# A two-layer decoder trunk on one core: expert weights in transfers of two pieces, and gathered tokens turned by VectorE instead of TensorE

## What is computed

```python
def swiglu(x, wg, wu, wd):
    return (jax.nn.silu(x @ wg) * (x @ wu)) @ wd

def moe(xn, w_router, wg, wu, wd):          # xn: 256 tokens x 2048, RMSNorm of x
    t = xn.reshape(-1, D)
    logits = (t @ w_router).astype(jnp.float32)
    top_vals, top_idx = lax.top_k(logits, TOP_K)            # 2 of 8
    gates = jax.nn.softmax(top_vals, axis=-1)
    comb = jnp.einsum('nk,nke->ne', gates, jax.nn.one_hot(top_idx, N_EXPERTS, dtype=jnp.float32))
    y = jnp.zeros_like(t)
    for e in range(N_EXPERTS):
        y = y + comb[:, e:e + 1].astype(t.dtype) * swiglu(t, wg[e], wu[e], wd[e])
    return y.reshape(B, S, D)
```

## Time and profile before

| | us |
|---|---|
| median of 3 runs | 1911.96 (1910.83 to 1913.84) |
| the profiled execution, its own time | 1910.22 |
| its span in the profile | 1908.5 |
| PE busy | 1897.8 (99% of the span) |
| DVE busy | 1440.1 (75%) |
| ACT busy | 1165.3 (61%) |
| POOL busy | 137.2 (7%) |
| HBM read and written | 495.33 MB and 13.64 MB, 267 GB/s over the span |

### The profile page before, as it was taken

How to read it: one execution, slowest core, us unless ns; L and a number is a source line. 1 busy time by engine, 2 the same in 40 slices (tenths; PEclk the granted TensorE clock), 3 DMA queues, 4 the chain that set the end, 5 groups by cost and what they waited for, 6 DMA issues and landing times.

```text
span 1908.5 us, 25748 instructions
## 1 busy us (share of the span) xinstructions
PE 1897.8 (99%) x8912; PEld 1580.5 (83%) x8912; DVE 1440.1 (75%) x1862; ACT 1165.3 (61%) x1490; POOL 137.2 (7%) x152
## 2 busy tenths in 40 slices
PE   9999999999999999999999999999999999999998
PEld 7888888888888888888888888888888888888887
DVE  8886677547764676566569678898988989888896
ACT  7656644434443444334545667888787878787885
POOL 8300000000000000000200010000000100010101
PEclk9999999999999999999999999999999999999999
DMA  9655566666666666665565468999999999999997
GB/s 358 195 159 164 177 193 193 191 196 192 194 191 195 192 195 190 196 193 187 185 186 167 145 217 337 374 397 385 396 386 398 379 398 378 403 378 403 375 396 258
DMA packets 141572, 510.13 MB, mean 267 GB/s; under 512 B 15937, under 2 KB 15953, under 8 KB 140081
## 3 DMA queue, kind: packets, MB, share of 16 engines
q1 hardware_dynamic: 134288, 486.64, 72.0%
q0 software_dynamic: 7200, 22.39, 4.6%
HBM read 495.33 MB, written 13.64 MB: 267 GB/s over the span
## 4 chain that ended last, share of the span: by engine, by line
PE 98%; DMA 1%; issue 0%; DVE 0%; ACT 0%; POOLq 0%; SPq 0%; DVEq 0%
PE main L637 31%; PE main L639 31%; PE main L638 31%; PE transpose L974 1%; PE transpose L655 1%; PE transpose L1014 0%; DMA raw_pieces<-in_ffn_moe 0%; PE transpose L957 0%; PE transpose L677 0%; DMA raw_pieces<-in_w_in 0%; PE transpose L732 0%; PE transpose L733 0%; PE transpose L731 0%; PE transpose L744 0%; PE spread L712 0%
## 5 line engine op out<-in xcount | busy, mean ns | idle before, releaser
L1423 DVE TENSOR_TENSOR w_low<-raw_pieces,w_high 128x1024 fp32r<-128x1024 f32 x919 | 1099.4, 1223 | 310.9 <-ACT w_high L1075 301.8
L1075 ACT ACTIVATE w_high<-raw_pieces 128x1024 fp32r<-128x1024 f32 x919 | 952.3, 1059 | 293.6 <-DMA raw_pieces<-in_ffn_dense 167.9
L637 PE MATMUL main<-w_high,xT_high 128*128 128x512 f32 (+1 forms) x1856 | 717.5, 387 | 0.3 <-DVE w_low L1544 0.2
L639 PE MATMUL main<-w_high,xT_low 128*128 128x512 f32 (+1 forms) x1856 | 709.7, 382 | 0.0
L638 PE MATMUL main<-w_low,xT_high 128*128 128x512 f32 (+1 forms) x1856 | 708.9, 382 | 0.0
L639 PEld LDWEIGHTS main<-w_high,xT_low 128*128 128x128 f32 x1856 | 348.8, 188 | 68.5
L637 PEld LDWEIGHTS main<-w_high,xT_high 128*128 128x128 f32 x1856 | 349.1, 188 | 66.3 <-issue 1.4
L638 PEld LDWEIGHTS main<-w_low,xT_high 128*128 128x128 f32 x1856 | 349.3, 188 | 65.3
L637 PE MATMUL main<-w_high,hT_high 128*128 128x512 f32 x832 | 329.9, 396 | 0.7 <-DVE hT_low L1839 0.6
L639 PE MATMUL main<-w_high,hT_low 128*128 128x512 f32 x832 | 324.6, 390 | 0.0
L638 PE MATMUL main<-w_low,hT_high 128*128 128x512 f32 x832 | 324.1, 390 | 0.0
(11 more groups left out here) (234 smaller groups left out, 820.3 us busy)
## 6 DMA issues: line engine op xcount, KB each, us to landing
raw_pieces<-in_ffn_moe SPq DMA_DIRECT2D x528, 512.0 KB, 6.3
raw_pieces<-in_ffn_dense SPq DMA_DIRECT2D x264, 512.0 KB, 3.5
raw_pieces<-in_w_in SPq DMA_DIRECT2D x96, 512.0 KB, 3.5
raw_pieces<-in_w_out SPq DMA_DIRECT2D x32, 512.0 KB, 3.6
x_resid<-in_x SPq DMA_DIRECT2D x4, 512.0 KB, 14.8
out_x<-x_resid POOLq DMA_DIRECT2D x4, 512.0 KB, 4.4
xn_rows<-token_major POOLq DMA_DIRECT2D x2, 1024.0 KB, 6.2
token_major<-in_x_t SPq DMA_DIRECT2D x1, 1024.0 KB, 9.7
```

What stands on the lines that cost most here:

```text
L637: pe.matmul(out_ap, lh[ls], rh[rs], start=first, stop=False)
L639: return pe.matmul(out_ap, ll[ls], rh[rs], start=False, stop=last)
L1075: act.activation(WH[:, piece % RING, :], RAWS[:, piece % RING, :], ACT.Copy).then_inc(high_done, 1)
L1423: dve.tensor_tensor(WL[:, piece % RING, :], RAWS[:, piece % RING, :], WH[:, piece % RING, :], ALU.subtract).then_inc(low_done, 1)
```

## The change

1. Expert weights lie in HBM in pairs (`in_pairs`, on the host), and SP loads two neighbouring slots of the ring with one transfer of 128 x 2048 (1 MB): pieces 0 and 1, 2 and 3, ... 8 and 9 of every 11, then piece 10 alone, so 36 transfers per expert instead of 66. A pair is issued when PE has finished both pieces that lay in its slots, and both pieces wait for its one semaphore (`landing`).
2. `XN` is stored with the feature index split the other way (`p t m k`: feature k * 128 + m at place m * 16 + k), so DVE writes it (L1632 before) and PE reads it for the first expert with a step of 16 elements. `xn_rows` has 4 rows of 512 for each token.
3. For experts 2 to 8, POOL issues four indirect DMAs instead of one. DMA i brings, for slots 32 i to 32 i + 31, the quarter rows such that each group of 32 partitions holds one quarter of the features. The row numbers need a second small product on PE at step 12 (`run_values_next` and a selection by slot within its run of 32) and a few small DVE instructions at step 8.
4. `gathered` and its evictions go. At steps 42, 44, 46 and 48 DVE turns 128 x 512 in 32 x 32 blocks with one `transpose` each, from `XG` into `xT_raw`, which lies in the memory of `xT_low`. At steps 49 and 50 ACT writes the high parts, 128 x 1024 each; two steps later DVE subtracts in place. PE waits for these halves at steps 58 and 62.
5. DVE computes the values for all experts once, in the first expert (`run_values`).

```diff
+E_QUARTER = {42: 0, 44: 1, 46: 2, 48: 3}
+E_HALF = {49: 0, 50: 1}
...
-        XN = TOK[:, 0:TILES * D].rearrange("p (t n) -> p t n", t=TILES)
+        XN = TOK[:, 0:TILES * D].rearrange("p (t m k) -> p t m k", t=TILES, k=KD)
...
+        def landing(piece):
+
+            n = piece - PASS[0]["piece"]
+            return raw_full[piece % RING - (1 if n >= 0 and n % RING % 2 else 0)]
...
                     for i in range(SLICE_PIECES):
-                        load(w[bass.ds(e, 1), i].rearrange("o p n -> (o p) n"), piece0 + i, e)
+                        turn, at = divmod(i, RING)
+                        if at % 2:
+                            continue
+                        count = min(2, RING - at)
...
+                        sp.wait_ge(used, e * SLICE_PIECES + (piece + count - RING))
+                        sp.dma_start(RAWS[:, slot:slot + count, :].rearrange("p s n -> p (s n)"), src).then_inc(landing(piece), 16)
...
-                    pool.indirect_dma_start(XG, None, ROWS[:, :], bass.IndirectOffsetOnAxis(ap=IDX[:, 0:1], axis=0)).then_inc(xg_in, 16)
+                    for i in range(RUNS):
+                        pool.indirect_dma_start(XG[:, i * NB:(i + 1) * NB], None, ROWS[:, :],
+                                                bass.IndirectOffsetOnAxis(ap=IDX[:, i:i + 1], axis=0)).then_inc(xg_in, 16)
...
-                            ins = pe.matmul(TP[k % 2][:, i * P:(i + 1) * P], XN[:, t, c * P:(c + 1) * P],
+                            ins = pe.matmul(TP[k % 2][:, i * P:(i + 1) * P], XN[:, t, :, c],
                                             SEL[:, t, :], start=t == 0, stop=t == TILES - 1)
...
-                def slot_values():
+                def slot_values(rows):
 
+                    for t in range(TILES if rows else 0):
+                        pe.matmul(U[0][:, 4:4 + RUNS], SELR[:, t, :], VRUN[:, t, :], start=t == 0, stop=t == TILES - 1)
...
-                def gathered(e, count, k, q):
...
-                        ins = pe.transpose(TP[k % 2][:, i * P:(i + 1) * P], XG[:, c * P:(c + 1) * P], IDN[:, :])
...
+                            if n_pass == 0:
+                                if (i - NEXT_GU) % 4 == 0:
+                                    pe.wait_ge(x_low_done, e * 2 + ((i - NEXT_GU) // 4 + 1))
...
+                        if i in E_HALF and more and n_pass == 0:
+                            half = slice(8 * E_HALF[i], 8 * E_HALF[i] + 8)
+                            act.wait_ge(x_turned, e * RUNS + RUNS)
+                            act.activation(XTH[:, half, 0:SLOTS], XTR[:, half, 0:SLOTS], ACT.Copy).then_inc(x_high_done, 1)
...
-                    dve.tensor_tensor(XN[:, t, cols], X[:, t, cols], GAIN[:, cols], ALU.mult).then_inc(xg_done, 1)
+                    chunks = slice(d * NB // P, (d + 1) * NB // P)
+                    dve.tensor_tensor(XN[:, t, :, chunks].rearrange("p m k -> p k m"), X[:, t, cols].rearrange("p (k m) -> p k m", m=P),
+                                      GAIN[:, cols].rearrange("p (k m) -> p k m", m=P), ALU.mult).then_inc(xg_done, 1)
...
+                        if i in E_QUARTER and more and n_pass == 0:
+                            q = E_QUARTER[i]
...
+                            dve.transpose(XTR[:, :, q * RUN:(q + 1) * RUN], XG[:, q * NB:(q + 1) * NB].rearrange(
+                                "p (r k) -> p k r", k=KD)).then_inc(x_turned, 1)
+                        if i - 2 in E_HALF and more and n_pass == 0:
+                            half = slice(8 * E_HALF[i - 2], 8 * E_HALF[i - 2] + 8)
+                            dve.wait_ge(x_high_done, e * 2 + (E_HALF[i - 2] + 1))
+                            dve.tensor_tensor(XTL[:, half, 0:SLOTS], XTR[:, half, 0:SLOTS], XTH[:, half, 0:SLOTS],
+                                              ALU.subtract).then_inc(x_low_done, 1)
```

More of the change, by code:

```diff
@@ L181, in expert_groups @@
     for i in range(SLICE_PIECES):
-        for kind, at in (("t", E_TURN), ("gather", E_GATHER if more else {}), ("st", expert_selt(more, n_pass))):
+        for kind, at in (("t", E_TURN), ("gather", E_GATHER if more and n_pass else {}), ("st", expert_selt(more, n_pass))):
             if i in at:
@@ L250, in trunk @@
         XTH = sb("xT_high", [P, KD, SEQ], F32R)
+        with ExitStack() as scratch:
+            XTR = sb("xT_raw", [P, KD, SEQ], F32, scratch)
         XTL = sb("xT_low", [P, KD, SEQ], F32R)
@@ L313, in trunk @@
         IOTA_I = SETUP[:, 17 * P:18 * P].bitcast(I32)
+        IOTAR_I = SETUP[:, 18 * P:19 * P].bitcast(I32)
         DQ = SETUP[:, 8 * P:11 * P]
@@ L340, in trunk @@
         TOKEN_I = sb("token_number_int", [P, TILES], I32)
-        IDX = sb("slot_tokens", [P, 1], I32)
+        IDX = sb("slot_rows", [P, RUNS], I32)
+        IOTAR = sb("iota_in_run", [P, SLOTS])
+        QUARTER = sb("row_quarter", [P, 1])
+        VRUN = sb("run_values_next", [P, TILES, RUNS])
+        SELR = CNT[:, 0:TILES * SLOTS].rearrange("p (t s) -> p t s", t=TILES)
+        VALR = NEGU[:, 0:TILES * RUNS * N_EXP].rearrange("p (t i e) -> p t i e", t=TILES, i=RUNS)
+        RUN_NO, IN_RUN, TOK4 = (NEGU[:, 64 + 16 * i:80 + 16 * i].rearrange("p (t e) -> p t e", t=TILES) for i in range(3))
         ZERO = sb("zero_row", [P, D // P])
@@ L1072, in high @@
             def high(piece, shift=0):
-                act.wait_ge(raw_full[piece % RING], shift * (16 * SLICE_PIECES // RING) + 16 * (piece // RING + 1))
+                act.wait_ge(landing(piece), shift * (16 * SLICE_PIECES // RING) + 16 * (piece // RING + 1))
                 act.activation(WH[:, piece % RING, :], RAWS[:, piece % RING, :], ACT.Copy).then_inc(high_done, 1)
@@ L1757, in gates, with run_values @@
                     link(dve.tensor_scalar(COMB[:, t, :], sel[:, t, :], MX[:, t:t + 1], None, ALU.mult))
+            def run_values():
+                link(dve.tensor_scalar(RUN_NO, SLOT[:, :, :], -0.5 - RUN / 2, 1.0 / RUN, ALU.add, ALU.mult))
+                link(dve.tensor_scalar(RUN_NO, RUN_NO, ROUND, None, ALU.add))
+                link(dve.tensor_scalar(RUN_NO, RUN_NO, -ROUND, None, ALU.add))
+                dve.scalar_tensor_tensor(out=IN_RUN, in0=RUN_NO, scalar=-float(RUN), in1=SLOT[:, :, :], op0=ALU.mult, op1=ALU.add)
+                for t in range(TILES):
+                    ins = dve.tensor_scalar(TOK4[:, t, :], CHOSEN[:, t, :], TOKEN[:, t:t + 1], float(RUNS), ALU.mult, ALU.mult)
+                link(ins)
+                for i in range(RUNS):
+                    ins = dve.scalar_tensor_tensor(out=VALR[:, :, i, :], in0=RUN_NO, scalar=float(i), in1=TOK4,
+                                                   op0=ALU.is_equal, op1=ALU.mult)
+                link(ins)
             def moe_pass(n_pass):
@@ L1877, in moe_pass @@
                     dve.wait_ge(idx_ready, 1)
-                    slot_values(1)
+                    slot_values(1, False)
+                    run_values()
                 with dve.Fori(0, N_EXP - 1) as e:
@@ L1910, in slice_pieces, with in_pairs @@
     return np.ascontiguousarray(np.concatenate([a, b, c], 1))
+def in_pairs(pieces):
+    s = pieces.shape[0]
+    turns = pieces.reshape(s, SLICE_PIECES // RING, RING, P, PW)
+    two = turns[:, :, :RING - 1].reshape(s, SLICE_PIECES // RING, RING // 2, 2, P, PW).transpose(0, 1, 2, 4, 3, 5)
+    return np.concatenate([two.reshape(s, SLICE_PIECES // RING, -1), turns[:, :, RING - 1].reshape(s, SLICE_PIECES // RING, -1)], 2)
 def dense_pieces(gate, up, down):
```

62 lines of the change are left out of this document (35 added, 27 removed).

## The result

The kernel before took 1911.39 us (median of 4 runs) in this comparison, the changed one **1942.07 us** (1940.20 to 1947.68): ratio 1.0164, with a 95% interval of 1.0152 to 1.0176. That is 30.7 us slower, where 1903.5 was forecast and 1924 was the end of the range. The profiled execution has a span of 1938.3 us, 29.8 more than before.

A forecast was written before the change was run, and what follows sets the result against it. PE, busy 99% of the span, was taken as the bound. From 1910.2 us, 10.7 less PE work, 1.7 of stall and 0.5 for the first expert gave 1901.7, forecast as 1903.5 us against the median; range 1900 to 1924.

The forecast's parts named there:

- Transfers: Expert weight stream: pairs land later but leads cover it; 0 taken, up to 5.6 us, plus 0.5 us for first expert.
- Rival C: Expert weights: pairs, or the transfers' rate, take the gain; 5.6 us, 1909 us, or 1912 if rate-bound; chance 0.09.
- The first expert's tokens: First expert's gather and DVE writes, read or written with a step: 0 taken, upper ends 7.4 and 1.1 us.
- B: First expert: PE's gather pays for its step, transposes don't; +7.4 us, 1910.9 us; chance 0.07 alone, 0.21 with A.
- DVE: Experts 2 to 8: four transposes at 0.71 us each, 0.86 with gap and overlap; PE stalls 1.7 us in all.
- A: Experts' DVE transposes pay for spread source, 1.21 us each; 1917.5 us; chance 0.17 alone, 0.21 with B.
- DVE's stretch: DVE from split of piece 56 to 67: 16.6 us plus four transposes, against 19.8 us that PE allows.
- the stall of 0.24 us: PE's wait per expert near the next expert's first piece: transposes take 3.44 us against 3.2 left.
- What PE gains: Step 12: two more small f32 products on PE cost 0.45 us per expert, 3.3 us; net 10.7 us less.
- the sum (1903.5): Whole kernel: 1910.2 - 10.7 + 1.7 + 0.5 = 1901.7 us, forecast as 1903.5 us against the median, 0.44% less.
- Three of the signs: Listed tests: transposes near 710 ns or 1.2 us, gather 7.4 us or up to twice, PE's expert waits over 5 us.
- the sign for C: Mid-expert: PE waits on `w_low` after transfers that ACT waited for would show that pairs take the gain.

The follow-up runs named there:

- `pairs_only`: The kernel before with only the paired 1 MB weight transfers added, tokens still turned by TensorE: 1944.05 us, ratio 1.0166.
- `after_single`: The changed kernel with its pairs taken back, 66 transfers of 512 KB per expert, spread token layout and DVE transposes kept: 1914.69 us, ratio 1.0013.
- `turn_before_split`: The change without pairs, tokens read side by side from POOL's reordered copies, DVE's `hT_low` subtraction moved ahead of its step's split: 1899.07 us, ratio 0.9930.

## Why the prediction was wrong

- **Transfers.** This step failed. It said that the first half of a pair comes "1.3 us later", that leads near 5 us are "cover enough", and took 0 to 5.6 us. The late issue, which the same paragraph names, was not added to the joint landing: the loop became 2.5 us longer for first halves and 2.3 for second ones, where it had 1.3 and 1.2. And the lead of 4.9 us is not free: the product and the turn stand behind DVE's split of a piece one to four ahead of PE's, so PE needs 1.4 to 5.5 us of that lead at each turn (the split of piece 21 stands before the product of block 1, which PE wants at piece 20). The cost was 27 us, five times the upper end. Rival C had the right place ("the pairs take the gain"), at a price of 5.6 us and a chance of 0.09. "PE never waited for a split" was true and no argument: in `pairs_only` PE hardly waits for a split either (1.6 us), but for what is queued behind one.
- **The first expert's tokens.** I took 0 and gave 7.4 and 1.1 as upper ends; measured are 6.8 for the gather and 0.6 per two writes on the chain, 2.1 with what they push. B, the upper end, came true.
- **DVE.** The transpose at 0.71 us held to 5 ns with neighbouring elements (705 ns), and A's premise was right for this kernel: 1.09 us, past the 1.03 at which I had it decide, near the upper end of 1.21. Its price was wrong: 1.7 us over the experts, not the 14 of A. Two things made it small. DVE's stretch was put too long: with 1.07 us per transpose the prediction's own sum gives 21.5 us from the split of piece 56 to that of 67 (16.6 and 4 x 1.22) and a stall of 1.7, and `after_single` took 20.4 and stalled 0.6. With 705 ns it was 19.4 on the mean for 20.0, and the stall of 0.24 us all but stayed away. (1503.19 and 1512.35 are the last matmuls of pieces 49 and 55; piece 50 starts at 1503.42, which puts 0.2 us more in hand.) And PE, late at the first piece, comes later to piece 48, where it waits 0.30 instead of 0.66: one wait takes the other's place.
- **What PE gains.** Right: pieces 50, 53, 56 and 59 are 0.56 us shorter each and the ones behind them 0.09 longer, 1.9 us in all for 2.0; the added product costs 0.44 to 0.46 for 0.47. The net is 1.5 us per expert, as forecast (1.53). `turn_before_split` has it, 92.4 to 92.7 for 94.12, with another 0.2 us from DVE's order.
- **A missing term.** I looked for DVE's critical stretch at pieces 56 to 67 and left out piece 48, where the trace had 0.13 us in hand. Without pairs or spread reads the sum (1903.5) would still have been 3 us low, for that wait: 0.66 us per expert.
- **Chances.** A and B share a cause, and that cause was real; I had given it 0.45 in all. With it and the pairs at the price of C the sum is 1924.9 + 5.6 = 1930.5, and the pairs' real price lies beyond.

Three of the signs worked: the transposes' 1090 ns, the gather's 14.24 us, and PE's waits over 5 us in sum (25 us). Experts 97.0 us apart were beyond every case (94.8 for A). And the sign for C, PE's waits on `w_low`, would have cleared the pairs: only 4.6 us of the waits in the experts carry that name, 18 carry `hT_low` and `h_blocks`.

## What to carry to other kernels

A ring of buffers is a loop: slot free, issue, landing, conversion, use. Before transfers are merged, write that loop down in microseconds and add both delays of the first half, the wait for the second slot and the joint landing; then look what small, urgent work stands in program order behind the conversion, because the wait will carry that name and not the transfer's. And before an order is called safe, look at every place where PE takes something from another engine for the distance between its end and PE's start: at one step 0.13 us were in hand, and the order there made the difference between a gain of 5 us and one of 13.

## What the runs showed of the hardware that I had not expected

- A step of 64 bytes in f32 reads costs PE's weight load 119 ns per 128 x 128 (311 for 192) and a product of the gather 106 ns (383 for 277); a DVE transpose of 128 x 512 costs 1074 to 1090 ns for 705. Two DVE writes of 128 x 512 with that step take 1.85 us for 1.28.
- Rows of 8 KB and of 4 KB in a 1 MB transfer: 1944.05 and 1944.71 us, no difference that shows.
- Dropping the indirect additions of the results to HBM gave 6.7 us (1899.88 for 1906.56) though PE was the bound in the profile. Half of it is the end of the kernel, where nothing waits for the last addition; in the experts landing took 5.4 us for 7.5, and PE's waits for `hT_low` fell from 4.4 to 3.3 us.
